# The second block's RMS norms moved behind their products, and the squares of its first two norms spread over the preceding down stage

## The reference, cut to what matters

```python
def rmsnorm(x, g):
    y = xf * lax.rsqrt(jnp.mean(xf * xf, axis=-1, keepdims=True) + EPS)
    return (y * g.astype(jnp.float32)).astype(x.dtype)
...
x = first_block(...)                      # ends in _rmsnorm(h, final_g)
for l in range(DEPTH):                    # DEPTH = 2
    h = rmsnorm(x, norm1_g[l])
    u = jnp.einsum('btd,de->bte', h, w_in[l])
    ...
    x = x + jnp.einsum('bte,ed->btd', mix, w_out[l])
    h2 = rmsnorm(x, norm2_g[l])
    a = jnp.square(jax.nn.relu(jnp.einsum('btd,df->btf', h2, w_up[l])))
    x = x + jnp.einsum('btf,fd->btd', a, w_down[l])
```

## Time and profile before

| | us |
|---|---|
| median of 3 runs | 3743.09 |
| lowest and highest | 3741.81, 3745.54 |
| the profiled execution | 3749.99 |
| its span | 3748.2 |
| PE busy in it | 3597.0 (96%) |
| POOL busy | 1490.6 (40%) |
| DVE busy | 1385.3 (37%) |
| ACT busy | 965.4 (26%) |

### The profile page before, as it was taken

The page is one execution under the profiler, slowest core; times in us unless marked ns, Lnnn a source line. Parts: engine busy times, 40 slices in busy tenths (PEclk is TensorE's granted clock), DMA queues, the critical chain, the costliest instruction groups (busy, mean ns, idle before and its releaser), DMA issues.

```text
span 3748.2 us, 41071 instructions
## 1 busy us (share of the span) xinstructions
PE 3597.0 (96%) x16200; PEld 2740.0 (73%) x16200; DVE 1385.3 (37%) x2572; ACT 965.4 (26%) x1205; POOL 1490.6 (40%) x521
## 2 busy tenths in 40 slices
PE   8999999799999999999999989989999999799999
PEld 7878777558887888755688866843888869437887
DVE  4454277624243422233210145752201267632010
ACT  2222222522223212303222233331212233312221
POOL 3445451025454545400354554401546445014453
PEclk9999998899999999999999989988999999799999
DMA  6434221025343433220223222101222212002222
...
DMA packets 53863, 360.58 MB, mean 96 GB/s; under 512 B 5968, under 2 KB 6352, under 8 KB 16592
## 3 DMA queue, kind: packets, MB, share of 16 engines
...
...
## 4 chain that ended last, share of the span: by engine, by line
PE 90%; DVE 6%; ACT 1%; issue 1%; DMA 1%; POOL 1%; SPq 0%; DVEq 0%; ACTq 0%; POOLq 0%
PE LP L459 80%; PE XB L459 9%; DVE S L1814 1%; PE LP L747 1%; DMA big<-w_ada 1%; PE XB L631 0%; ACT E L1060 0%; DVE tmp L1936 0%; DVE st L1934 0%; POOL wk L1481 0%; ACT sq L1060 0%; DVE wk L1834 0%; DVE gain L1651 0%; DVE stat L1826 0%; POOL w_lo L1423 0%
## 5 line engine op out<-in xcount | busy, mean ns | idle before, releaser
L1423 POOL TENSOR_TENSOR w_lo<-ring,w_hi 128x2048 fp32r<-128x2048 f32 (+1 forms) x263 | 1122.9, 4270 | 682.8 <-ACT w_hi L1060 682.0
L459 PE MATMUL LP<-u_hi,w_hi 128*128 128x512 f32 x2480 | 992.9, 400 | 21.2 <-ACT u_hi L1060 17.0
L459 PE MATMUL LP<-u_hi,w_lo 128*128 128x512 f32 x2480 | 980.5, 395 | 0.0
L459 PE MATMUL LP<-u_lo,w_hi 128*128 128x512 f32 x2480 | 937.6, 390 | 0.0
L459 PE MATMUL LP<-big_r,w_hi 128*128 128x512 f32 x2432 | 749.6, 389 | 1.2 <-POOL w_lo L1423 1.2
L1060 ACT ACTIVATE w_hi<-ring 128x2048 fp32r<-128x2048 f32 (+1 forms) x263 | 468.7, 1782 | 813.9 <-PE LP L459 726.1
L459 PEld LDWEIGHTS LP<-u_hi,w_hi 128*128 128x128 f32 x2480 | 475.5, 192 | 137.3 <-issue 39.1
L459 PEld LDWEIGHTS LP<-u_hi,w_lo 128*128 128x128 f32 x2480 | 474.9, 192 | 102.2
L459 PEld LDWEIGHTS LP<-u_lo,w_hi 128*128 128x128 f32 x2480 | 467.0, 188 | 95.2 <-issue 0.5
L459 PEld LDWEIGHTS LP<-big_r,w_hi 128*128 128x128 f32 x2432 | 455.9, 188 | 95.6 <-issue 1.3
L459 PE MATMUL LP<-big_r,w_lo 128*128 128x512 f32 x1216 | 473.2, 389 | 0.0
...
## 6 DMA issues: line engine op xcount, KB each, us to landing
...
```

The source lines that it names most:

```text
L459: return pe.matmul(o, lhsT=lhsT, rhs=rhs, start=start, stop=stop)
L1423: gp.tensor_tensor(w_lo[:, slab % RING, 0:width], ring[:, slab % RING, 0:width], w_hi[:, q % 2, 0:width].bitcast(F32), ALU.subtract).then_ ...
```

## The change

It concerns the four places ahead of `in0`, `up0a`, `in1` and `up1a`, and what follows from them.

- The input of the products is now h times the gain, without the root. ACT (`late_chunk`) writes `u_hi` straight from h as each chunk becomes final, then squares the chunk. DVE (`late_input`) makes `u_lo` from h, gain and `u_hi`. u is not written any more. The running sum of squares moves to `rstd`, since `u_hi` now fills `wk` early.
- PE runs `total_sum` inside slab 0, between the `u_hi` and the `u_lo` products, and `spread` behind slab 0.
- DVE copies the spread root to R (`tabs[:, 3, :]`) and multiplies by it as it takes results out of LP: the columns of `in` but for queries and keys, the values of `inv` (there by one factor per token), and the `up` stage, where DVE takes max(x, 0) · R first and ACT squares `tmp` afterwards. Queries and keys keep their own norm; its mean is multiplied by R twice before the root and its reciprocal by R once.
- Ahead of `in0` both norms are taken at once. ACT makes two squares of each chunk, of h and of h times `final_g`; for chunks 0 to 5 it does so behind the slabs of `dn11b`, and POOL keeps two sums (`rstd` and `rt`) there. DVE works out both roots from both sums, PE spreads both (the first into `XB[3]`), and DVE scales h by the first behind slab 0 of `in0`.
- The early load of the square root's table is gone from these places, and the `up{l}a` stages are no longer loops of two turns but written out.

```diff
+        R = tabs[:, 3, :]
+        mean4, first4 = st[:, 0:4], st[:, 8:12]
+        def square_home(c, late, second=False):
+            if second:
+                return tabs[:, 2 + c % 2, :] if c else rt[:, :]
+            return sq[:, c % 2, :] if c else rstd[:, :] if late else sqa
...
-            return 4 if pl.slab == 0 else n_ada if 0 < n_ada < n else None
+            return 4 if pl.slab == 0 or name in ("up0a", "up1a") else n_ada if 0 < n_ada < n else None
...
+                        if fresh.late:
+                            total_sum(fresh.late)
...
+                    if k == 0 and fresh is not None and fresh.late:
+                        spread(fresh.late)
...
-            def total_sum():
+            def total_sum(late=0):
                 if pl.norm:
                     pe.wait_ge(s("rt_ready"), pl.norm)
-                pl.got("squares_summed")
-                for b in range(NB):
-                    mm(XB[1][:, b:b + 1], sqa[:, blk(b)], cc("ones", 0, 1), start=b == 0, stop=False)
-                pl.got("h_squared", DC)
-                for b in range(NB):
-                    last = mm(XB[1][:, b:b + 1], sq[:, (DC - 1) % 2, blk(b)], cc("ones", 0, 1), start=False, stop=b == NB - 1)
+                for i in range(2 if late == 2 else 1):
+                    pl.got("seconds_summed" if i else "squares_summed")
+                    for b in range(NB):
+                        mm(XB[1][:, 4 * i + b:4 * i + b + 1], square_home(0, late, i)[:, blk(b)], cc("ones", 0, 1),
+                           start=b == 0 and i == 0, stop=False)
+                for i in range(2 if late == 2 else 1):
+                    pl.got("seconds" if i else "h_squared", DC)
+                    for b in range(NB):
+                        last = mm(XB[1][:, 4 * i + b:4 * i + b + 1], square_home(DC - 1, late, i)[:, blk(b)],
+                                  cc("ones", 0, 1), start=False, stop=b == NB - 1 and i == (late == 2))
                 last.then_inc(s("total_ready"), 1)
                 pl.norm += 1
-            def spread():
+            def spread(late=0):
                 pe.wait_ge(s("rstd_ready"), pl.norm)
+                if late == 2:
+                    for b in range(NB):
+                        mm(XB[3][:, blk(b)], first4[:, b:b + 1].to_broadcast([P, P]), cc("ident"))
                 for b in range(NB):
                     last = mm(XB[0][:, blk(b)], root4(b).to_broadcast([P, P]), cc("ident"))
                 last.then_inc(s("rstd_spread"), 1)
...
+            def late_norm(twice=False):
+                fresh = Fresh(u_hi2, pl.ur, 2 if twice else 1)
+                pl.ur += DC
+                return input_of(u_hi2), fresh
...
-            total_sum()
-            spread()
             for l in range(DEPTH):
-                src, fresh = norm(u_hi2)
+                src, fresh = late_norm(twice=l == 0)
...
+            def late_chunk(c, gains, twice):
+                f(u_hi2[:, c, :], h[:, c, :], ACT.Copy, scale=gains[:, c:c + 1]).then_inc(s("u_high"), 1)
+                if c >= 3:
+                    act.wait_ge(s("sq_added"), pl.seen.get("sq_added", 0) + c - 2)
+                f(square_home(c, True), h[:, c, :], ACT.Square).then_inc(s("h_squared"), 1)
+                if twice:
+                    if c >= 3:
+                        act.wait_ge(s("second_added"), c - 2)
+                    f(square_home(c, True, True), h[:, c, :], ACT.Square, scale=sp_("final_g", c)).then_inc(s("seconds"), 1)
+            def final_chunk(k):
+                if k < DC - 2:
+                    g = pl.group + k
+                    act.wait_ge(s(f"lin_taken{g % 2}"), g // 2 + 1)
+                    if k == 0:
+                        act.wait_ge(s("total_ready"), pl.seen.get("total_ready", 0))
+                        pl.got("gain_ready")
+                    late_chunk(k, gain, True)
+            def late_rms(gains, per=1, cut_at=(7,), twice=False):
+                act.wait_ge(s("total_ready"), pl.seen.get("total_ready", 0))
+                for c in range(DC - 2 if twice else 0, DC):
+                    for j, chunk in enumerate(cut_at):
+                        if chunk == c:
+                            high(pl.cut + j)
+                    pl.chunk_final(c, per)
+                    late_chunk(c, gains, twice)
+                pl.passed("sq_added", DC - 2)
+                for q in range(len(cut_at), 2):
+                    high(pl.cut + q)
+                pl.got("total_ready")
+                if pl.norm:
+                    act.wait_ge(s("rstd_ready"), pl.norm)
+                f(rt4, XB[1][:, 0:NB], ACT.Sqrt, scale=1.0 / D, bias=cc("eps")).then_inc(s("rt_ready"), 1)
+                pl.norm += 1
+                if twice:
+                    pl.got("second_mean")
+                    f(mean4, mean4, ACT.Sqrt, bias=cc("eps")).then_inc(s("second_root"), 1)
...
-                    pl.got("qk_summed")
-                    f(qk_rows(i), XB[0][0:8, :], ACT.Sqrt, scale=1.0 / P, bias=cc("eps")[0:8, :])\
+                    pl.got("qk_means")
+                    f(qk_rows(i), qk_rows(i), ACT.Sqrt, scale=1.0 / P, bias=cc("eps")[0:8, :])\
...
-                    def relu(k, it):
-                        act.wait_ge(s("lin_done"), at(s0 + k + 1, it, RING))
-                        act.wait_ge(s("h_cut"), at(low0 + k - 1, it, RING))
+                    def square(k, it):
                         p = (g0 + k) % 2
-                        f(tmp[:, p, :], LPF[p], ACT.Relu).then_inc(s("silu_done"), 1)
-
-                    layer(f"up{l}{part}", relu)
+                        act.wait_ge(s(f"lin_taken{p}"), at((g0 + k) // 2 + 1, it, RING // 2))
+                        f(tmp[:, p, :], tmp[:, p, :], ACT.Square).then_inc(s("silu_done"), 1)
+                    layer(f"up{l}{part}", square)
...
+            def late_square(c, twice):
+                gp.wait_ge(s("h_squared"), pl.seen.get("h_squared", 0) + c + 1)
+                o = square_home(0, True)
+                gp.tensor_tensor(o, o, square_home(c, True), ALU.add).then_inc(s("sq_added"), 1)
+                pl.got("sq_added")
+                if twice:
+                    gp.wait_ge(s("seconds"), c + 1)
+                    o = square_home(0, True, True)
+                    gp.tensor_tensor(o, o, square_home(c, True, True), ALU.add).then_inc(s("second_added"), 1)
+                    pl.got("second_added")
+            def late_squares(cut_at=(7,), twice=False):
+                for c in range(DC - 2 if twice else 1, DC):
+                    if c == DC - 1:
+                        gp.nop().then_inc(s("squares_summed"), 1)
+                        if twice:
+                            gp.nop().then_inc(s("seconds_summed"), 1)
+                    for j, chunk in enumerate(cut_at):
+                        if chunk == c:
+                            rest(pl.cut + j)
+                    if c == DC - 1:
+                        break
+                    late_square(c, twice)
+                pl.passed("h_squared", DC)
+                for q in range(len(cut_at), 2):
+                    rest(pl.cut + q)
...
+            def final_square(k):
+                if 1 <= k < DC - 2:
+                    late_square(k, True)
...
+            def late_input(gains, twice=False):
+                for c in range(DC):
+                    pl.got("u_high")
+                    stt(u_lo[:, c, :], h[:, c, :], gains[:, c:c + 1], u_hi2[:, c, :].bitcast(F32), ALU.mult, ALU.subtract)\
+                        .then_inc(s("u_ready"), 1)
+                dve.wait_ge(s("rt_ready"), pl.norm + 1)
+                pl.norm += 1
+                if twice:
+                    link(dve.reciprocal(first4, rt4))
+                    link(tt(mean4, first4, first4, ALU.mult))
+                    stt(mean4, XB[1][:, NB:2 * NB], 1.0 / D, mean4, ALU.mult, ALU.mult).then_inc(s("second_mean"), 1)
+                    pl.got("second_root")
+                    link(dve.reciprocal(mean4, mean4))
+                    tt(root4(0, NB), mean4, first4, ALU.mult).then_inc(s("rstd_ready"), 1)
+                else:
+                    dve.reciprocal(root4(0, NB), rt4).then_inc(s("rstd_ready"), 1)
+                pl.got("rstd_spread")
+                link(dve.tensor_copy(R, XB[0][:, :]))
...
-            scale_in(h, sp_("final_g", 0, DC))
-            dve.wait_ge(s("u_scaled"), pl.tu)
             for l in range(DEPTH):
                 init = 0.8 - 0.6 * math.exp(-0.3 * l)
-                scale_in(u, sp_("norm1", l * DC, DC), u_hi2)
+                late_input(sp_("norm1", l * DC, DC) if l else gain, twice=l == 0)
...
+                    pl.got("qk_summed")
+                    link(tt(qk_rows(i), XB[0][0:8, :], R[0:8, :], ALU.mult))
+                    tt(qk_rows(i), qk_rows(i), R[0:8, :], ALU.mult).then_inc(s("qk_means"), 1)
                     pl.got("qk_root")
-                    dve.reciprocal(qk_rows(i), qk_rows(i)).then_inc(s("qk_recip"), 1)
```

(15 more changed lines are left out.)

58 lines of the change are left out of this document (26 added, 32 removed).

## The result

| | before | after |
|---|---|---|
| median of the runs, us | 3744.43 (7 runs) | 3715.74 (7 runs) |
| lowest and highest | 3741.81, 3754.15 | 3697.95, 3723.92 |
| the profiled execution | 3749.99 | 3705.63 |
| its span, granted clock | 3748.2, 0.963 | 3703.8, 0.971 |

The ratio after to before is 0.991, with a 95% interval from 0.9889 to 0.9931: 26 to 42 us off, 34 in the middle (the plain medians differ by 28.7). The kernel is faster, and both the median and the interval's times lie inside the predicted range. The forecast of 42.7 us off was too high: it just misses the interval. The interval says how far chance in the timed runs can have moved the ratio. The two profiled executions lie 44.4 us apart, more than the ratio says, and this has to be explained too.

What follows compares the result with a forecast made beforehand. PE, busy 96% of the span, was taken as the bound, losing time by waits and lower clock at four seams. Gains 17.1 + 10.4 + 6.7 + 9.3 - 0.8 = 42.7 us gave 3700.4 us; range 3695 to 3721.

Steps and rivals of the forecast that it cites:

- B to D: Last product ahead of `up0a`, `in1`, `up1a` to that stage's slab 1: 14.1 us each, gaining 10.4, 6.7, 9.3.
- Seam A: Last product of `dn11b` to slab 1 of `in0`, two norms: 19.5 us with the wait, gaining 17.1.
- The wait for `w_lo`: At seam A, PE waits 2.2 us for POOL's weight cut, which ends at 2187.5.
- the 3.63 us for the 16 `u_lo` products: Slab 0 of each seam: 16 products at the full clock, 0.227 us each; at A they cover the roots.
- the rival of the lower clock: Clock falls in all four seams: 15.0 us lost, time 3715.4 us; chance 0.14.
- The root's chain at A: Table load, two roots and short DVE operations take 3.0 us, under a cover of 3.63 us.
- The up stages: Behind a late norm the weight cut ends at 12.3, wanted at 12.0; 0.4 us each, 0.8 in all.
- The slower rival: Up chain grows by 1.8 us, each of 32 up slabs overruns by 1.4, the gain is lost; chance 0.03.
- The lock of POOL and DVE at k = 4: In `in0` and `in1`, DVE's last product starts 0.25 us before POOL's cut: taken as free, otherwise 5.2 us in all.
- Waiting fronts: PE reaches slab 0 without `u_hi`; half the gain of B, C and D lost, 13.2 us: 3713.6; chance 0.08.
- the same gain on the median: The 42.7 us off the profiled 3749.99 also taken off the timed median 3743.09, giving 3700.4.
- held-up evictions: Rival inside the stages: lock at k = 4 (5.2 us) plus up chain (9.6), 14.8 together: 3715.2; chance 0.12.

Runs made afterwards that it cites:

- cut_first: Changed kernel with slab 0's weight cut on ACT and POOL ahead of chunk 6 instead of chunk 7 at seam A; median 3707.46 us, ratio 0.9892.
- fillers: Two kernels: 2 or 4 products added to the changed kernel ahead of each wait for probabilities in the second block's attention; medians 3708.77 and 3712.62 us.
- sums_first: Changed kernel with the products that sum the squares put ahead of slab 0's `u_hi` products again; median 3735.41 us, ratio 0.9967.
- after_again: The changed kernel run once more, unchanged; median 3711.94 us (5 runs), ratio to before 0.9906.

## Why the prediction was right, and where it was off

**What bounds the kernel, and the seams: right.** The prediction said 19.5, 14.1, 14.1 and 14.1 us; the trace shows 20.7, 13.4, 13.5 and 13.4, a gain of 44.4 us instead of 43.5. Two terms of B to D were too dear. The 16 small products take 1.70 us in B (2597.45 to 2599.15), not 2.1, and the spread 0.81, not 1.1. PE at seam B, timeline:

```profile
2597.45 0.95 PE L468 MATMUL XB<-cst,rstd 128*128 128x1 f32 x8
2598.26 1.03 PE L468 MATMUL XB<-cst,sq 128*128 128x1 f32 x8
2599.15 3.88 PE L468 MATMUL LP<-u_lo,w_hi 128*128 128x512 f32 x16
2602.87 1.05 PE L468 MATMUL XB<-cst,st 128*128 128x128 f32 x8
2603.68 0.48 PE L468 MATMUL LP<-u_hi,w_hi 128*128 128x512 f32 x1
```

The prediction had taken the end of a row for the start of the next. Rows of products overlap at their ends, so a sum must be made from start to start.

**Seam A: the wait right, one term missed.** The wait for `w_lo` was predicted with 2.2 us and is 2.70, by the chain that was named: POOL ends the sums of chunk 6, then the cut of slab 0 (2175.61 to 2180.16). The step that failed there is the 3.63 us for the 16 `u_lo` products. They take 5.33. The stretches of the seam behind the `u_hi` products:

```profile
2187.76:2191.24 3.48, 3.48 (x33) 3.48 (x32) 1.94 (x3) 0.00 (x0) 0.00 (x0) 1.00 0.00 0
2191.24:2196.57 5.33, 5.33 (x18) 4.24 (x18) 0.84 (x5) 0.56 (x2) 0.00 (x0) 0.68 0.00 0
2196.57:2198.28 1.71, 1.71 (x17) 1.70 (x16) 0.00 (x0) 1.45 (x1) 0.00 (x0) 1.00 0.33 48
```

The clock falls to a mean of 0.68 behind the 3.48 us of one-column products and costs 1.7 us. The same row is in all eight traces of kernels with this order and a wait of 2.7 us or none at A (5.32 to 5.34 us). It is not the wait of 2.70 us that does it: `cut_first` has no wait and the same row (2189.56 to 2194.88, 5.32 us). In B and D 1.70 us of such products left the clock at 1.00. Fewer of them at A were not tried, so that it is their number and nothing else of this seam is likely, not shown. So the rival of the lower clock was real at one of four seams, at 1.7 of its 15 us, and by its "small products use one column each", not by its idle time. (Its "gaps of under a second each" at C are gaps of under a microsecond: 0.78 and 0.57 us.)

**The root's chain at A: right, by more than said.** The reciprocals and what follows end at 2193.02, and PE wants the roots at 2196.57. DVE and ACT there, timelines:

```profile
2191.72 0.18 DVE L1744 RECIPROCAL st<-st 128x4 f32<-128x4 f32 x1 [2.02 <-ACT st L1087]
...
2192.86 0.16 DVE L1749 TENSOR_TENSOR st<-st 128x4 f32<-128x4 f32 x1
...
2182.37 1.28 ACT L1087 ACT_TABLE_LOAD   x1
2191.42 0.27 ACT L1087 ACTIVATE st<-XB,cst 128x4 f32<-128x4 f32 x1 [7.76 <-PE XB L468]
```

The table load was reckoned on the chain with 1.28 us; it runs at 2182.37, right behind the weight cut, while ACT waits for the sums. Nothing of it is on the path.

**The up stages: right.** Predicted 0.8 us for both (12.3 less 12.0 is 0.3 in each, not the 0.4 that is written), measured 0.95 (337.80 instead of 337.29 and 345.43 instead of 344.99). The chain behind slab 0 of `up0a`, DVE, ACT, DVE, POOL:

```profile
2604.68 1.22 DVE L2424 SCALAR_TENSOR_TENSOR tmp<-LP,tabs 128x1024 f32<-128x1024 f32 x1
...
2605.94 1.06 ACT L1087 ACTIVATE tmp<-tmp 128x1024 f32<-128x1024 f32 x1 [6.35 <-DVE tmp L2424]
...
2607.03 0.70 DVE L2426 TENSOR_SCALAR big_r<-tmp 128x1024 fp32r<-128x1024 f32 x1 [1.13 <-ACT tmp L1087]
...
2610.19 4.62 POOL L1482 TENSOR_TENSOR w_lo<-ring,w_hi 128x2048 fp32r<-128x2048 f32 x1
```

The cut ends at 2614.81, 11.1 us behind the end of slab 0, where slab 2 wants it after some 10.9. The slower rival, an up chain longer by 1.8 us in each slab, did not come: the chain is late once, in the slab behind the norm.

**The lock of POOL and DVE at k = 4: met, and free.** The added product and POOL's cut do collide, and DVE came first. DVE and POOL of `in0` at k = 4 in after, timelines:

```profile
2273.27 0.68 DVE L2212 TENSOR_TENSOR big<-big,tabs 8x512 f32<-8x512 f32 x1
...
2273.61 4.83 POOL L1482 TENSOR_TENSOR w_lo<-ring,w_hi 128x2048 fp32r<-128x2048 f32 x1 [7.80 <-ACT w_hi L1087]
```

The product keeps its 0.68 us, and POOL's cut, which begins 0.34 us behind it, takes 4.83 us in place of 4.62; in `in1` it is the same. So the one that started first went ahead, as the prediction has it for this case, and the later one paid 0.2 us instead of 0.4. PE doesn't feel it: it has no wait between slab 1 and the mixer. From the start of slab 1 to the last product of `inv` it takes 195.7 us in the four traces of before and of kernels made from it, and 195.8 to 195.9 in the ten others. The forecast of the order rested on a distance of 0.25 us; that it held by so little is luck.

**Waiting fronts: absent.** PE's `u_hi` products start without idle time at B, C and D.

**The step that failed: the same gain on the median.** The prediction took the gain of 42.7 us, worked out in the seams, over to the median as it was, and let the clock rival act in the seams alone. It held the mixers to be unchanged because no instruction of them is. But in the second block a mixer took anything between 137.6 and 146.9 us, at a clock between 0.84 and 0.76, in the twelve traces without fillers. The scatter of 2 us that the lower end of the range used came from three runs; twenty runs of the same kernel scatter by 16 us. That the median came into the range is therefore partly luck. Its room had been made for the lower clock and for held-up evictions in the seams and stages, and the measured 3715.7 is by chance the time of both these rivals (3715.4 and 3715.2), which the trace rules out but for the 1.7 us at A. In the first pair of traces the mixers with `wo` took 6.9 us of the gain back; in `cut_first` the second mixer took all 3 us back that the seam had gained; in the trace of `sums_first` the two mixers together were 5.6 us shorter than in `after_again`, so that a loss of 20.7 in the seams is 15.2 from A to the end. What stays open: the timed runs say 34 us and the sum of the seams and the stages without mixers and `wo` some 43. From A to the end the traces of after are shorter by 36.5 us than the first of before and by 43.4 than the second, and the 36.5 lie within the interval of 26 to 42. So the difference of 9 is of the size of this effect, and it is not shown that it is all of it: a trace shows one execution. Nor is it shown why the first mixer takes 143.2 to 144.0 us in seven traces of after and of kernels made from it, wherever it starts (205 to 222 us behind the start of A), but 138.6 in `sums_first`, and 137.9 in both of before.
